# Hybrid decoder step on one core: early weights, conditioning units and idle products put in a new order

## The chip, the cores and the metric

The kernel runs on 1 core of a Trainium2 chip. The metric is the device time of one execution in microseconds (us). Times before: 1947.58 median of 3 runs (1947.49 to 1947.77).

## The reference, cut to what matters

One layer of a decoder trunk on 512 prompt tokens and 8 sample tokens (520 in all), D_MODEL 2048, all in float32. The change touches only the first step: the conditioning of the normalised input, and the first columns of the input projection.

```
def _modulate(x, c, g_norm, w_ada, b_ada):
    mod = c @ w_ada + b_ada
    shift, scale, gate = jnp.split(mod, 3, axis=-1)
    h = _rms(x, g_norm) * (1 + scale[:, None, :]) + shift[:, None, :]
    return h, gate

def _project_in(h, w_in, pos):
    z = h @ w_in
    ...
    q, k, v, qi, ki, wi, ga, u, gb, ma, mb = parts
```

`c` has 9 rows (1 prompt, 8 samples); `w_ada` is 2048 x 6144, `w_in` 2048 x 13456. Behind it come the sparse attention with its indexer, the pooling mixer, the gated merge, the output projection and the final RMS norm.

## The kernel before, in words

**Products in three parts.** A float32 product with a weight tile is done as three products of a faster format: weights high x input high, weights high x input low, weights low x input high. So each 2048 x 128 weight tile (1 MB) passes three steps: a DMA into `raw[p]` (`load`, L344), ACT's cast to `whi[p]` (`hi`, L657), and GpSimd's (POOL's) subtraction into `wlo[p]` (`lo`, L529). There are two such buffers, p = 0 and 1. The input stands in `act_hi` and `act_lo` (16 slices of 128 rows, 520 columns). TensorE's helper `tile` (L1611) runs the products into `acc[p]`.

**The front.** Four token tiles are transposed on TensorE (`token_columns`, L1686) into `H`. Meanwhile `w_ada`'s shift and scale parts (32 units of 1 MB) flow through a ring of SBUF slots. `cond_unit(u)` (L1624) multiplies unit u with the 9 rows of `c`. Four units make a chunk of 512 columns; the order is ADA_CHUNKS: chunks 0 to 3 are scale, 4 to 7 shift. After a chunk ACT copies its sums out of PSUM (`mod_rows`, L695), TensorE turns them into columns (`mod_columns(c)`, L1657), and VectorE and ACT make four slices of the input: VectorE scales `H` (L1047), ACT casts to `act_hi` (L704), VectorE subtracts to `act_lo` (L1032). `scale_rows` (L1694) and `table_columns` (L1645, L1646) prepare the row factors and small tables.

**Early tiles.** While the units stream in, four tiles of the projection (columns of `mb`) are computed from the scaled input without shift, as `early tile` 0 to 3; a later correction adds what the shift makes of them. Tiles 0 and 1 are done in quarters: `early_quarter(e, g)` takes the four slices of group g (24 products), and waits for `act_lo` slice by slice. Tile 0 uses buffers p = 1, tile 1 buffers p = 0. Tiles 2 and 3 follow in one piece each (`tile(*early_at(2), ...)`), with the later units between their parts.

**Slots.** The first units lie in slots that overlay the early tiles' buffers: slot 0 is `raw[0]`, slot 2 `whi[0]`, slot 4 `wlo[0]`. The units from LATE on use five late slots, four of them over the token tiles (`x_tok`), one over `xs`; so SP waits for the transposes (`xT_done`) and ACT's squares (`ss_ready`) ahead of unit LATE, and each later unit waits until the former one of its slot is used (`ring_done`).

**Order.** All queues are written out by hand. SP issues, in one queue: constants, x, units 0 and 1, early tile 0's weights, units 2 and 3 (FIRST_RING has three slots, so unit 3 is the first late one), then it waits for unit 2 to be used and issues early tile 1's weights, then units 4 to 31 with the further early weights between. TensorE's program is one list: units 0 to 2, `scale_rows`, `table_columns`, unit 3, `mod_columns(0)`, then units 4 to 19 with the quarters behind the units that `quarters_after` names; `mod_columns(1)` to `(3)` stand directly behind units 8, 12 and 16. Each engine works through its list in order.

Of the kernel before, what the change touches and what calls it, by code (L numbers as in the profile page):

```python
# [56 lines left out]
ADA_CHUNKS = [4, 5, 6, 7, 0, 1, 2, 3]  # L57
RING = 6
ADA_UNITS = 4 * len(ADA_CHUNKS)
FIRST_RING, LATE_RING = (2, 4, 0), 4  # L60
LATE = len(FIRST_RING)


# [53 lines left out]
def build(nc, t, out):  # L117
# [11 lines left out]
    def at(name, off, shape, dt=F32):  # L129
        size = int(np.prod(shape[1:])) * (2 if dt == BF16 else 4)  # L130
        assert off + size <= 229368 - BASE, (name, off, size)
        return nc.alloc_sbuf_tensor_at(name, shape, dt, offset=BASE + off)
# [9 lines left out]
    ident = at("ident", A0, [P, P])  # L142
# [148 lines left out]
    acc = [ctx.enter_context(nc.psum_tensor(f"acc{p}", [P, 2, 512], F32)) for p in range(2)]  # L291
# [17 lines left out]
    S = sem  # L309
# [5 lines left out]
    def cols(w, c):  # L315

        return w[:, bass.ds(c, P)].rearrange("(k p) n -> p k n", p=P)
# [9 lines left out]
    def early_at(e):  # L327

        return ((e + 1) // 2, 1 - e % 2)
# [8 lines left out]
    def _(sp):  # L338
        def load(q, p, src, first=False):
            if not first:  # L340
                sp.wait_ge(lo_ready[p], q - 1 + p)
            k, n = src.shape[1], src.shape[2]
            dst = raw[p][:, 0:k * n].rearrange("p (k n) -> p k n", n=n)
            sp.dma_start(dst, src).then_inc(raw_landed[p], 16)  # L344

        def load_ada(u):

            former = [v for v in range(u) if RING_AT[v] == RING_AT[u] or RING_SEM[v] == RING_SEM[u]]
            if former:
                sp.wait_ge(S("ring_done"), former[-1] + 1)  # L350
            sp.dma_start(ring[RING_AT[u]][:].rearrange("p (k n) -> p k n", n=512),
                         quarter(w_ada, u % 4, 512 * ADA_CHUNKS[u // 4])).then_inc(stage_landed[RING_SEM[u]], 16)

        def load_early(e, first=False):
            load(*early_at(e), cols(w_in, C_MB + P * e), first=first)
# [9 lines left out]
        sp.dma_start(pgi[:], t["page_table"].rearrange("(o b) n -> o b n", o=1).broadcast_to([P, NB, PAGES])  # L365
                     ).then_inc(S("pages_landed"), 16)
        for u in range(ADA_UNITS):
            if u == 2:
                load_early(0, first=True)
            if u == LATE:  # L370
                sp.wait_ge(S("xT_done"), 8)
                sp.wait_ge(S("ss_ready"), 4)
            if u == LATE + 1:
                sp.wait_ge(S("ring_done"), LATE)
                load_early(1, first=True)
            if u == LATE + LATE_RING:
                sp.wait_ge(S("front_T"), 2)
                sp.wait_ge(S("ss_ready"), 5)
            if u == 17:
                load_early(2)  # L380
            if u == 20:
                load_early(3)
            if u == 27:
                load(Q_A, 1, cols(w_in, C_KI))
            load_ada(u)
# [1187 lines left out]
    def _(pe):  # L1573
        mm = nc.tensor.matmul
# [44 lines left out]
        def cond_unit(u):  # L1619

            c = u // 4
            pe.wait_ge(stage_landed[RING_SEM[u]], 16 * (RING_USE[u] + 1))
            for k in range(4):
                last = mm(ps[32 * k:32 * k + 32, c % 2, :], cWide[:, 4 * (u % 4) + k, :],  # L1624
                          ring[RING_AT[u]][:, k * 512:(k + 1) * 512],
                          start=(u % 4 == 0), stop=(u % 4 == 3))
            last.then_inc(S("ring_done"), 1)

        def early_quarter(e, g):

            tile(*early_at(e), 0, parts=S("act_lo_ready"), free=False, ks=range(4 * g, 4 * g + 4))
# [11 lines left out]
        def table_columns():  # L1643
            pe.wait_ge(S("tables_landed"), 8 * 16)
            tr(ps[:, 3, 16:64], rows_b[:], ident[0:48, 0:48])  # L1645
            tr(ps[:, 3, 64:88], rows_gs[:], ident[0:24, 0:24]).then_inc(S("front_T"), 1)  # L1646

        def mod_columns(c):

            pe.wait_ge(S("mod_rows"), c + 1)  # L1650
            if c == 0:
                pe.wait_ge(S("xs_ready"), 1)
            else:
                pe.wait_ge(S("H_ready"), max(4 * c - 7, 1))
            part, g = divmod(ADA_CHUNKS[c], 4)
            for m in range(4):
                last = mm(modT[g][:, part, m, :], modb[c % 2][:, m * P:(m + 1) * P], sum4, start=True, stop=True)  # L1657
            last.then_inc(S("mod_T"), 1)
# [31 lines left out]
        def scale_rows():  # L1690
            pe.wait_ge(S("xT_act"), 4)
            pe.wait_ge(S("diag_ready"), 5)
            for i in range(4):
                mm(acc[0][:, 0, i * P:(i + 1) * P], ones[:], diag[:, i, :], start=True, stop=True)  # L1694
            mm(acc[0][:, 1, 0:NB], ones[0:NB, :], diagS[:], start=True, stop=True).then_inc(S("front_T"), 1)

        def unit(u):
            if u % 4 == 0 and u >= 8:
                pe.wait_ge(S("mod_rows"), u // 4 - 1)
            cond_unit(u)  # L1700
            if u % 4 == 0 and u > 4:
                mod_columns(u // 4 - 1)

        token_columns(0)
# [1 line left out]
        for i in range(1, 4):  # L1706
            token_columns(i)
        pe.wait_ge(S("front_set"), 2)
        for u in range(3):
            unit(u)  # L1710
        scale_rows()
        table_columns()
        unit(3)
        mod_columns(0)
        pe.wait_ge(S("xT_dve"), 4)
        quarters_after = {4: [(0, 0)], 6: [(1, 0)], 9: [(0, 1)], 12: [(1, 1)], 14: [(0, 2)], 16: [(1, 2)],
                          17: [(0, 3), (1, 3)]}
        for u in range(4, 20):
            unit(u)
            for e, g in quarters_after.get(u, ()):  # L1720
                early_quarter(e, g)
# [458 lines left out]
```

## Time and profile before

| What | Value |
| --- | --- |
| Median of the runs | 1947.58 us |
| Profiled execution: its own time | 1951.26 us |
| Profiled execution: span | 1949.4 us |
| TensorE matmul busy (PE) | 1906.1 us, 98% |
| VectorE (DVE), ScalarE (ACT), GpSimd (POOL) busy | 1009.5, 546.1, 910.4 us |
| Chain that ended last | PE 93%, of it line L1611 70% |
| Mean granted clock of TensorE | 0.991 |

The busy share is a mean over stages with different limits; the stretches of the trace tell them apart. PEclk is the granted TensorE clock as a share of 2.4 GHz: 1.00 or 0.50, which is 1.2 GHz. A value in brackets behind an instruction is the idle time of its engine before it, and what ended it. PE's float32 products stand as two records each.

### The profile page before, as it was taken

To read this page: it belongs to the slowest core of one execution; us is meant where nothing else is said; L and a number is where in the kernel's file an instruction comes from. 1 tells how busy PE (TensorE), PEld (TensorE's weight loads), DVE (VectorE), ACT (ScalarE), POOL (GpSimd) and SP (SyncE) were. 2 spreads that over 40 slices of the span, in tenths; PEclk is the share of its full clock that TensorE was granted. 3 is DMA by queue.
4 is the path that set the end of the run, shared out by engine and by line. 5 is a ranking of instruction groups with operands and counts; after the bars stand their busy time and mean duration, and the time that the engine had idled before them with its cause. 6 is when DMAs were issued, how large, how long until landed. Compare 5 with 4: busy or idle time off the path is not lost.

```text
span 1949.4 us, 34601 instructions
## 1 busy us (share of the span) xinstructions
PE 1906.1 (98%) x14468; PEld 1771.6 (91%) x14468; DVE 1009.5 (52%) x1529; ACT 546.1 (28%) x751; POOL 910.4 (47%) x760
## 2 busy tenths in 40 slices
PE   6999999999999999999999999999999999999997
PEld 4679999988999999999999999999999999887775
DVE  4358886677787778774444675425011411142223
ACT  4332322443333333332222121212222411131223
POOL 1135555555454545453444343444665444334442
PEclk7999999999999999999999999999999999999999
DMA  9994434443333232324233353326475655543333
GB/s 322 342 312 107 108 104 123 139 133 115 88 79 97 75 93 74 97 77 132 72 88 88 98 148 102 97 76 173 133 235 174 186 182 172 180 144 131 98 104 131
DMA packets 328257, 264.44 MB, mean 136 GB/s; under 512 B 8747, under 2 KB 275175, under 8 KB 326839
## 3 DMA queue, kind: packets, MB, share of 16 engines
q1 hardware_dynamic: 314719, 232.42, 40.2%
q10 hardware_dynamic: 8320, 13.80, 2.6%
q0 software_dynamic: 5120, 16.77, 2.5%
q8 instruction: 79, 1.29, 0.3%
q14 instruction: 19, 0.16, 0.0%
HBM read 250.89 MB, written 12.54 MB: 135 GB/s over the span
## 4 chain that ended last, share of the span: by engine, by line
PE 93%; DVE 2%; DMA 2%; SPq 1%; ACT 1%; issue 1%; POOL 0%; DVEq 0%; POOLq 0%; ACTq 0%
PE acc L1611 70%; PE ps L2120 9%; PE ps L1876 1%; DMA ring<-in_w_ada 1%; PE ps L1751 1%; PE ps L1892 1%; PE ps L1624 1%; PE acc L1590 1%; PE ps L1864 1%; PE ps L2049 1%; PE acc L2111 1%; PE ps L1797 1%; PE ps L1939 1%; PE acc L1596 1%; PE ps L1807 0%
## 5 line engine op out<-in xcount | busy, mean ns | idle before, releaser
L529 POOL TENSOR_TENSOR wlo<-raw,whi 128x512 fp32r<-128x512 f32 (+1 forms) x612 | 789.2, 1321 | 818.4 <-ACT whi L657 818.4
L1611 PE MATMUL acc<-act_hi,whi 128*128 128x260 f32 (+1 forms) x3520 | 753.1, 290 | 8.0 <-DVE act_lo L1032 3.0
L1611 PE MATMUL acc<-act_hi,wlo 128*128 128x260 f32 (+1 forms) x3520 | 741.3, 287 | 0.0
L1611 PE MATMUL acc<-act_lo,whi 128*128 128x260 f32 (+1 forms) x3520 | 740.1, 287 | 0.0
L1611 PEld LDWEIGHTS acc<-act_hi,whi 128*128 128x128 f32 x3520 | 552.4, 189 | 34.3 <-issue 23.4
L1611 PEld LDWEIGHTS acc<-act_lo,whi 128*128 128x128 f32 x3520 | 550.9, 189 | 0.7
L1611 PEld LDWEIGHTS acc<-act_hi,wlo 128*128 128x128 f32 x3520 | 551.2, 189 | 0.0
L657 ACT CAST whi<-raw 128x2048 fp32r<-128x2048 f32 (+1 forms) x153 | 279.2, 1825 | 950.9 <-PE acc L1611 749.2
L2120 PE MATMUL ps<-whi,act_hi 128*128 128x512 f32 x256 | 102.1, 399 | 0.0
L2120 PE MATMUL ps<-whi,act_lo 128*128 128x512 f32 x256 | 101.1, 395 | 0.0
L2120 PE MATMUL ps<-wlo,act_hi 128*128 128x512 f32 x256 | 101.0, 394 | 0.0
L1477 DVE SCALAR_TENSOR_TENSOR big<-big,acc 128x520 f32<-128x520 f32 x16 | 11.1, 695 | 155.9 <-PE acc L1611 155.9
L567 POOL CAST k_part<-kT 128x512 fp32r (+1 forms) x16 | 9.8, 612 | 135.8 <-PE ps L1892 124.8
L2120 PEld LDWEIGHTS ps<-whi,act_hi 128*128 128x128 f32 x256 | 48.0, 188 | 21.1 <-issue 10.1
L2120 PEld LDWEIGHTS ps<-whi,act_lo 128*128 128x128 f32 x256 | 48.0, 188 | 11.3
L2120 PEld LDWEIGHTS ps<-wlo,act_hi 128*128 128x128 f32 x256 | 48.1, 188 | 11.0
L814 ACT ACTIVATE accS<-ps,misc 128x128 f32<-128x128 f32 (+1 forms) x64 | 32.9, 527 | 80.8 <-DVE misc L1254 80.8
L767 ACT COPY kiTc<-ps 128x512 f32<-128x512 f32 x32 | 35.0, 1093 | 67.1 <-PE ps L1797 67.1
L1346 DVE SCALAR_TENSOR_TENSOR big<-e_back,acc 128x520 f32<-128x520 f32 (+1 forms) x12 | 8.4, 696 | 84.9 <-PE acc L1611 84.9
L1611 PE MATMUL acc<-pool_hi,whi 128*128 128x260 f32 x256 | 52.0, 284 | 0.0
L1611 PE MATMUL acc<-pool_hi,wlo 128*128 128x260 f32 x256 | 51.4, 282 | 0.0
L1611 PE MATMUL acc<-pool_lo,whi 128*128 128x260 f32 x256 | 51.4, 282 | 0.0
(322 smaller groups left out, 2121.9 us busy)
## 6 DMA issues: line engine op xcount, KB each, us to landing
raw<-in_w_in SPq DMA_DIRECT2D x105, 1024.0 KB, 5.8
ring<-in_w_ada SPq DMA_DIRECT2D x32, 1024.0 KB, 11.4
raw<-in_w_a_proj SPq DMA_DIRECT2D x16, 1024.0 KB, 8.0
gate_unit<-in_w_ada SPq DMA_DIRECT2D x16, 1024.0 KB, 7.1
raw<-in_w_out SPq DMA_DIRECT2D x16, 1024.0 KB, 5.1
raw<-in_w_b_proj SPq DMA_DIRECT2D x16, 512.0 KB, 4.3
x_tok<-in_x_prompt SPq DMA_DIRECT2D x4, 1024.0 KB, 9.1
att_dram<-silu_ga ACTq DMA_DIRECT2D x16, 256.0 KB, 2.6
```

The source lines that it names most:

```text
L529: return nc.gpsimd.tensor_tensor(wlo[p][:, a:b], raw[p][:, a:b], whi[p][:, a:b].bitcast(F32), ALU.subtract)
L657: nc.scalar.copy(whi[p][:, 0:n], raw[p][:, 0:n]).then_inc(hi_ready[p], 1)
L767: nc.scalar.copy(kiTc[u % 4][:].rearrange("p (c r) -> p r c", r=4), ps[:, 2 if u else 3, :].rearrange("p (r c) -> p r c", r=4)).then_inc(S ...
L814: last = nc.scalar.activation(prob[:, OFF[b]:OFF[b] + w], ps[:, bank, c:c + w], ACT.Exp, bias=nmq[:, b:b + 1], scale=ATT_SCALE, accum_out= ...
L1590: mm(o, whi[p][:, k * P:(k + 1) * P], x[:, k, s], start=(k == 0 and x is hi_), stop=False)
L1596: last = mm(o, wlo[p][:, k * P:(k + 1) * P], hi_[:, k, s], start=False, stop=(k == KT - 1))
L1611: last = mm(o, w, x[:, k, s], start=(k == 0 and n == 0), stop=(k == kt - 1 and n == 2))
L1624: last = mm(ps[32 * k:32 * k + 32, c % 2, :], cWide[:, 4 * (u % 4) + k, :], ring[RING_AT[u]][:, k * 512:(k + 1) * 512], start=(u % 4 == 0) ...
L1751: last = mm(ps[:, b - 1, 0:(b + 1) * P], qis[p][:, x, (b - 1) * P:b * P], kis[:, y, 0:(b + 1) * P], start=(n == 0), stop=(n == 2))
L1797: last = tr(ps[:, 2 if u else 3, r * P:(r + 1) * P], kib[u % 3][:, r * P:(r + 1) * P], ident[:])
L1864: last = tr(ps[:, n // 4, (n % 4) * P:(n % 4 + 1) * P], prob[:, OFF[qb] + kb * P:OFF[qb] + (kb + 1) * P], ident[:])
L2120: last = mm(ps[:, i, :], x, w, start=(k == 0 and n == 0), stop=(k == KT - 1 and n == 2))
```

## The change

Slot 0 goes from the first units' list, so that units 0 and 1 lie in slots 2 and 4 and unit 2 is the first late one. SP issues early tile 0's weights ahead of unit 0 and early tile 1's weights behind unit 3; its wait for unit 2 goes, since `raw[0]` no longer holds a unit. POOL's wait (`ring_done`, LATE) ahead of tile 1's low part is now for two units. TensorE's list is rewritten up to unit 8. `keep_running(n)` does n products of the identity with itself into columns of a PSUM bank that nothing reads: 33 in all. TensorE's wait for VectorE's last token copy (`xT_dve`) moves ahead of the first of them. `scale_rows` and `table_columns` stand behind unit 1, `mod_columns(1)` behind unit 7 and twelve idle products, and the quarters behind other units.

```diff
@@ -57,7 +57,7 @@
 ADA_CHUNKS = [4, 5, 6, 7, 0, 1, 2, 3]
 RING = 6
 ADA_UNITS = 4 * len(ADA_CHUNKS)
-FIRST_RING, LATE_RING = (2, 4, 0), 4
+FIRST_RING, LATE_RING = (2, 4), 4
 LATE = len(FIRST_RING)
 
 
@@ -365,13 +365,12 @@
         sp.dma_start(pgi[:], t["page_table"].rearrange("(o b) n -> o b n", o=1).broadcast_to([P, NB, PAGES])
                      ).then_inc(S("pages_landed"), 16)
         for u in range(ADA_UNITS):
-            if u == 2:
+            if u == 0:
                 load_early(0, first=True)
             if u == LATE:
                 sp.wait_ge(S("xT_done"), 8)
                 sp.wait_ge(S("ss_ready"), 4)
-            if u == LATE + 1:
-                sp.wait_ge(S("ring_done"), LATE)
+            if u == 4:
                 load_early(1, first=True)
             if u == LATE + LATE_RING:
                 sp.wait_ge(S("front_T"), 2)
@@ -1694,11 +1693,15 @@
                 mm(acc[0][:, 0, i * P:(i + 1) * P], ones[:], diag[:, i, :], start=True, stop=True)
             mm(acc[0][:, 1, 0:NB], ones[0:NB, :], diagS[:], start=True, stop=True).then_inc(S("front_T"), 1)
 
+        def keep_running(n, spare=acc[1]):
+            for _ in range(n):
+                mm(spare[:, 1, 384:512], ident[:], ident[:], start=True, stop=True)
+
         def unit(u):
             if u % 4 == 0 and u >= 8:
                 pe.wait_ge(S("mod_rows"), u // 4 - 1)
             cond_unit(u)
-            if u % 4 == 0 and u > 4:
+            if u % 4 == 0 and u > 8:
                 mod_columns(u // 4 - 1)
 
         token_columns(0)
@@ -1706,16 +1709,29 @@
         for i in range(1, 4):
             token_columns(i)
         pe.wait_ge(S("front_set"), 2)
-        for u in range(3):
-            unit(u)
+        unit(0)
+        pe.wait_ge(S("xT_dve"), 4)
+        keep_running(4)
+        unit(1)
         scale_rows()
         table_columns()
+        unit(2)
+        keep_running(4)
         unit(3)
+        keep_running(5)
         mod_columns(0)
-        pe.wait_ge(S("xT_dve"), 4)
-        quarters_after = {4: [(0, 0)], 6: [(1, 0)], 9: [(0, 1)], 12: [(1, 1)], 14: [(0, 2)], 16: [(1, 2)],
-                          17: [(0, 3), (1, 3)]}
-        for u in range(4, 20):
+        unit(4)
+        keep_running(8)
+        early_quarter(0, 0)
+        unit(5)
+        unit(6)
+        keep_running(6, acc[0])
+        unit(7)
+        keep_running(6, acc[0])
+        mod_columns(1)
+        early_quarter(1, 0)
+        quarters_after = {9: [(0, 1)], 11: [(1, 1)], 13: [(0, 2)], 15: [(1, 2)], 17: [(0, 3), (1, 3)]}
+        for u in range(8, 20):
             unit(u)
             for e, g in quarters_after.get(u, ()):
                 early_quarter(e, g)
```

## Rows read from the trace of the kernel before

**Rows 1.** Page, part 1: busy us, share of the span, instructions.

```profile
PE 1906.1 (98%) x14468; PEld 1771.6 (91%) x14468; DVE 1009.5 (52%) x1529; ACT 546.1 (28%) x751; POOL 910.4 (47%) x760
```

**Rows 2.** Stretches: length, PE, PEld, DVE, ACT, POOL busy, clock, DMA share, GB/s.

```profile
25.40:45.70 20.30, 13.46 (x57) 7.95 (x58) 8.28 (x22) 6.08 (x7) 4.94 (x4) 0.50 0.96 329
...
52.70:56.00 3.30, 3.30 (x17) 3.28 (x16) 0.00 (x0) 0.00 (x0) 0.00 (x0) 0.50 1.05 387
...
62.90:66.20 3.30, 3.30 (x16) 3.00 (x15) 2.51 (x4) 1.22 (x2) 0.00 (x0) 0.50 1.05 388
66.30:93.80 27.50, 27.39 (x224) 19.30 (x223) 12.27 (x24) 9.19 (x13) 1.68 (x2) 1.00 0.98 316
93.80:144.20 50.40, 50.11 (x404) 39.38 (x404) 26.57 (x39) 17.57 (x25) 20.82 (x15) 1.00 0.98 330
```

**Rows 3.** Timeline, 0 to 60 us: start, length, instruction, [idle before <- releaser].

```profile
18.04 1.94 PE L1686 MATMUL acc<-ident,x_tok 128*128 128x128 f32 x16 [1.10 <-ACT H L687]
...
20.77 1.06 PE L1624 MATMUL ps<-ring,cWide 128*32 128x512 f32 x8 [0.79 <-DMA ring<-in_w_ada]
...
23.43 1.07 PE L1624 MATMUL ps<-ring,cWide 128*32 128x512 f32 x8 [1.59 <-DMA ring<-in_w_ada]
...
26.77 1.90 ACT L657 CAST whi<-raw 128x2048 fp32r<-128x2048 f32 x1 [3.47 <-DMA raw<-in_w_in]
...
29.51 1.94 PE L1624 MATMUL ps<-ring,cWide 128*32 128x512 f32 x8 [5.02 <-DMA ring<-in_w_ada]
...
31.51 0.37 SPq L344 DMA_DIRECT2D raw<-in_w_in  x1
...
40.94 1.94 PE L1624 MATMUL ps<-ring,cWide 128*32 128x512 f32 x8 [2.03 <-DMA ring<-in_w_ada]
```

**Rows 4.** Chain that ended last, 18 to 57 us: start, length, what.

```profile
31.45 2.01 PE acc L1694 x8
...
34.47 1.91 PE ps L1624 x8
...
36.40 0.59 ACT modb L695
...
37.04 1.89 PE ps L1657 x8
...
51.57 4.67 PE acc L1611 x24
```

**Rows 5.** Timeline of PE at two waits (49 to 52, 60 to 63 us).

```profile
51.57 0.51 PE L1611 MATMUL acc<-act_hi,whi 128*128 128x260 f32 x2 [2.44 <-POOL wlo L529]
...
62.31 0.48 PE L1611 MATMUL acc<-act_hi,whi 128*128 128x260 f32 x2 [2.24 <-DVE act_lo L1032]
```

**Rows 6.** Chain that ended last, 56 to 95 us.

```profile
58.09 1.00 PE ps L1657 x8
...
61.47 0.71 DVE act_lo L1032
...
62.31 4.84 PE acc L1611 x24
...
73.83 1.85 PE ps L1624 x16
75.68 3.06 PE acc L1611 x24
```

**Rows 7.** Timeline of DVE: third and fourth low slice of group 1.

```profile
64.02 1.47 DVE L1032 TENSOR_TENSOR act_lo<-H,act_hi 128x520 fp32r<-128x520 f32 x2
```

**Rows 8.** Timeline of PE in the attention: one f32 product, then the next.

```profile
715.27 0.38 PE L1877 MATMUL ps<-reluP,vcur 128*128 128x128 f32 x2
715.49 0.39 PE L1888 MATMUL ps<-kT,qiT 128*128 x2
```

**Rows 9.** Timeline of PE: first product of early tile 2.

```profile
93.70 0.50 PE L1590 MATMUL acc<-act_hi,whi 128*128 128x260 f32 x2
```

**Rows 10.** Tile ring, the transfer that SP issued at 76.9: issue to landing.

```profile
DMA to landing us min/median/max: 12.5/12.5/12.5
```

## The prediction, made before the changed kernel ran

> **What bounds the kernel now.** I read part 1 of the page first: TensorE (PE) is busy 98% of the span [rows 1], so a change counts only where it moves PE's own sequence. The change lies in the first 94 us, so next came the table of stretches [rows 2]. The reader is to see two things there. From 25.4 to 45.7 PE ran at a granted clock of 0.50, the lower level of 1.2 GHz, and again in two short stretches up to 66.2. From 66.3 on it runs at 2.4 GHz and is busy 27.39 of 27.50 us, then 50.11 of 50.40. So after 66.3 PE neither waits nor is slowed, though the DMA share there is 0.98: transfers and PE run nearly level, and PE is the one that sets the end. All that can be won lies between 20.0 us, where the last token transposes end, and 66.3, plus what the new order does up to 93.70, the first product of the third early tile [rows 9], which I take as the finish line: what follows it is the same program, with PE full, and I carry a shift there through to the end one for one.
>
> The timeline then shows the losses. PE waits for units 0, 1, 2 and 4 (0.79, 1.59, 5.02 and 2.03 us) [rows 3], for the low part of the second early tile (2.44) and for the first low activation slice of group 1 (2.24) [rows 5]. The 5.02 us stand because the first early tile's weights lie between units 1 and 2: the units start at 20.77 and 23.43, the cast of those weights at 26.77, unit 2 at 29.51. The 2.03 us stand because SP issues the second early tile's weights at 31.51 only, when unit 2 is done [rows 3].
>
> **Prices.** From the rows at 2.4 GHz: two units 1.85, so 0.93 each; mod_columns 0.99; a quarter 3.06 [rows 6]. At 1.2 GHz: unit 1.94 [rows 3], scale_rows with table_columns 3.02 (31.45 to 34.47), mod_columns 1.89 [rows 4]. An idle product is a 128x128 f32 product: at 2.4 GHz such a product in the attention takes 0.22 from its start to the next [rows 8]; at 1.2 GHz four in scale_rows take 2.01, 0.50 each [rows 4]. There are 33 of them, 7.3 or 16.5 us of PE work that was not there. The chain through VectorE: call T0 to T3 the ends of mod_columns 0 to 3. Before, T1 is 59.09 and the first low slice ends at 61.47 + 0.71, T1 + 3.1 [rows 6]; the fourth at 64.02 + 1.47, T1 + 6.4 [rows 7]. A quarter of that group can't start before T + 3.1 nor end before T + 6.4 + 0.8 (its last fourth) = T + 7.2. The second early tile's low part is ready at 51.57 with T0 = 38.93, T0 + 12.6 [rows 4, 5].
>
> **The change part by part, in order of time.**
>
> *First early weights ahead of unit 0.* They take 3.3 us of the stream (23.43 to 26.77) and a unit 2.7. Moved to the front, they put unit 0 at 24.1 and unit 1 at 26.8; unit 2 stays at 29.5, unit 3 lands near 32.2 as before. PE now idles 4.1 us before unit 0, and no more between units.
>
> *Units 0 to 3 with idle products.* At 1.2 GHz: unit 0 to 26.0, 4 idle products 28.0, unit 1 29.9, scale_rows and table_columns 33.0. Where the clock rises no row of before can say, since idle products are not in it. Bounds: at 2.4 GHz throughout, unit 3 is done 33.1, its copy (0.59 and some 0.1 of signals) 33.8, 5 idle products 34.2, T0 = 35.2. At 1.2 throughout, unit 2 34.9, 4 idle 36.9, unit 3 38.8, 5 idle 41.3, T0 = 43.2. I take a rise at 33.0, after 9 us without a gap: unit 2 33.9, idle 34.8, unit 3 35.7, idle 36.8, T0 = 37.8, that is 1.1 earlier than before. The copy is hidden behind the 5 idle products.
>
> *Second early weights behind unit 3, no wait for unit 2.* SP's wait goes. In the stream these weights then follow unit 3 at once: unit 4 at 32.2 + 3.3 + 2.7 = 38.2 or, if they take 1 us more, 39.2; I take 38.7 in place of 40.94. Queued behind on SP are units 4 to 31, which move forward by the same 2.2 us. That they need their ring slots freed by PE is no limit: five slots are ahead.
>
> *Unit 4, 8 idle products, quarter (0,0).* Unit 4 and the idle products take 2.7 us at 2.4 GHz, 5.9 at 1.2; PE has just done mod_columns and waited about 1 us for unit 4, so I can't tell and take the middle, 4.3: 43.0. All low slices of group 0 are there by T0 + 6.4 = 44.2, so the quarter runs through, to 46.1.
>
> *Units 5 to 7, two times 6 idle products, mod_columns(1).* All landed. 2.8 of units, 2.6 of idle products on the path, 1.0: T1 = 52.5. Of each six idle products only the second's hides anything, the copy before mod_columns (0.7). Before, T1 was 59.09, but with quarter (1,0) and unit 8 done; with these (3.06 + 0.93) the new order stands at 56.5, so 2.6 ahead for equal work.
>
> *Quarter (1,0) behind T1.* Its low part is ready at T0 + 12.6 = 50.4: the wait of 2.44 is gone. With units 8 and 9 it also fills the time up to T1 + 3.1, so quarter (0,1) no longer waits 2.24. It ends at 60.5; units 10, 11, quarter (1,1), unit 12, mod_columns(2): T2 = 67.3.
>
> *Quarters after 11, 13, 15 in place of 12, 14, 16.* Here the order takes something back. Before, quarter (1,1) and units 13, 14 stood between mod_columns(2) and quarter (0,2), 4.8 us of work over a chain of 3.1. Now only unit 13 does (0.9): PE waits 2.2 us for the first low slice, then goes at VectorE's pace. The same between mod_columns(3) and quarter (0,3), which has only unit 17 before it. Before, quarter (0,1) stood just so, behind unit 9: it ended at 67.15, T1 + 8.06 [rows 6], more than 7.2 because the clock fell to 0.50 in it [rows 2]. I take 8.06 twice: quarter (0,2) to 75.4, units 14, 15 and quarter (1,2) 80.3, unit 16 and mod_columns(3) T3 = 82.2, quarter (0,3) 90.3, (1,3) 93.3, units 18 and 19 95.2. Without the stall these two quarters would end at T + 4.0, so the new order costs 4.1 each.
>
> A rule speaks against this price. In both waits of before (2.44 and 2.24 us) the granted clock was 0.50 in the stretch after them [rows 2, 5]. The Trainium skill (TensorE: Matmul & The Clock Gate, section "Why this matters for your kernels") warns of longer gaps between bursts than these. By that rule the waits of 2.2 us would leave the clock up, and the quarters end at T + 7.2: 93.5 in place of 95.2. The rows disagree with it here, and I go by the rows.
>
> **The sum.** 95.2 - 93.70 = +1.5 us. Won: 2.6 up to T1. Lost: two stalls, less the one stall of before. On the profiled execution (span 1949.4, its own time 1951.26) that gives 1952.8. The median of the runs shown, 1947.58, lies 3.7 below the profiled one; the same shift gives 1949.1.
>
> **The rivals.**
>
> *The clock stays down until quarter (0,0) (slower).* T0 = 43.2, unit 4 45.1, 8 idle products 49.1, the quarter as long as the one before (4.67 [rows 4]) 53.8, then 6.4 to T1 at 60.2, 7.7 later than in the sum: +9.2, 1956.8. For it: before, PE worked from 29.51 to 36.38 without a gap and the clock stayed at 0.50 [rows 2 to 4]; nearly the same instructions now follow in another order. Against it: the idle products are denser than table_columns or mod_columns, and dense quarters brought the clock back each time. It decides from T1 = 54.9 on, where the shift passes 3.9 us. Half of it (only unit 4 and its idle products at 1.2, 1.6 more) gives 1950.7, still no change.
>
> *The clock holds everywhere.* T0 = 35.2, unit 4 and idle products to 41.4, quarter (0,0) 41.4 to 44.6, T1 = 51.0, and both stalls end at T + 7.2: 1.5 + 1.7 less than the sum, 92.0, -1.7: 1945.9.
>
> *The stream sets the end (faster).* If PE only followed its transfers, closing the hole would count in full. Unit 19 was issued at 76.9 and landed 12.5 later [rows 10], at 89.4. Without holes, 16 units of 2.7 and two early loads of 3.3 behind unit 3 put it at 32.2 + 43.2 + 6.6 = 82.0, 7.4 earlier. That would be 1940.2. For it: DMA share 0.98 [rows 2]. Against: unit 19 was used one unit ahead of 93.70, at 92.8, 3.4 after it landed, and PE's work up to there doesn't shrink.
>
> *The moved load does nothing.* If SP, held by a full queue, still gets unit 4 in at 40.9, that is 2.2 later in the sum: T1 = 54.7, 1951.3.
>
> **How the numbers follow.** Two thousandths of the time, 3.9 us, is about what a measurement can tell from no change: 1943.7 to 1951.5. The sum and its milder clock variants, 1947 to 1951.3, hold 0.62; the clock that holds 0.12; the load without effect 0.03; the clock down until the quarter or most of the way 0.16; the stream 0.07. So faster 0.07, same 0.75, slower 0.18 (the slow clock, and a little of the upper end of the sum). The range reaches from 1945.6, just below the case with the clock up, to 1952.8, about halfway to the slow-clock case.
>
> **What would show it.** Unit 0 starting near 24 and unit 4 near 38.7, SP's load of the second early tile issued before 31.5. T0 near 38 and T1 near 52.5. Waits of about 2.2 us on act_lo ahead of the quarters behind units 13 and 17, with a granted clock of 0.50 behind them, and none ahead of the quarter behind unit 9. The third early tile starting near 95.2. It is wrong if the clock up to 43 is other than said, if those two waits are missing, or if something after the finish line gives a shift back.

## The result and the profile after

Measured side by side, 14 runs each: 1953.35 us median (1951.63 to 1955.55) for the changed kernel, 1948.49 (1946.66 to 1950.85) for the kernel before; ratio 1.0021 with a 95% interval of 1.0014 to 1.0029, so 2.7 to 5.7 us slower. Applied to the 1947.58 of the prediction, the ratio gives 1951.7, inside its range of 1945.6 to 1952.8. The forecast was +1.5, in the class of no change (two thousandths); the measurement lies at the border of that class, on the slow side. The profiled execution took 1952.72 with a span of 1950.9, both 1.5 above the profiled execution before; its third early tile starts at 96.52 in place of 93.70 [rows 9], 2.8 later.

The stretches of the changed kernel (length, busy time of the engines, granted clock, DMA share, GB/s), to be read beside [rows 2]:

```profile
26.30:36.20 9.90, 7.96 (x62) 4.93 (x59) 4.47 (x15) 0.67 (x2) 4.95 (x4) 1.00 1.10 353
36.40:43.00 6.60, 4.96 (x22) 3.30 (x23) 4.88 (x8) 4.30 (x5) 0.39 (x1) 0.50 1.05 387
43.20:70.30 27.10, 25.64 (x211) 18.06 (x209) 8.38 (x19) 4.36 (x8) 4.42 (x4) 1.00 1.03 374
70.50:77.10 6.60, 6.01 (x28) 5.47 (x32) 3.69 (x6) 1.63 (x3) 0.00 (x0) 0.50 1.11 343
77.40:87.40 10.00, 7.76 (x66) 4.72 (x59) 3.33 (x8) 1.83 (x3) 0.00 (x0) 1.00 1.03 320
87.60:90.80 3.20, 3.20 (x15) 3.06 (x15) 2.60 (x5) 1.25 (x2) 0.00 (x0) 0.50 1.05 387
91.00:144.00 53.00, 53.00 (x434) 41.19 (x433) 22.11 (x35) 19.71 (x26) 20.04 (x16) 1.00 0.92 296
```

The clock is up through the first units, which it was not before. Three stretches stand at 1.2 GHz: one over unit 4 and its eight idle products (unit 4 ran at 1.2 GHz before too), and one around each of two waits at quarters (0,2) and (0,3), which is new. From 91 on PE is full without a gap. What PE waited for in the first 200 us (total, times, longest):

```profile
PE ps L1623 <- DMA ring<-in_w_ada: 6.5, 4, 3.1
PE acc L1610 <- DVE act_lo L1031: 5.5, 3, 2.2
```

The wait of 2.4 us for the low part of the second early tile is gone [rows 5]; the waits for act_lo have grown from one long one to two. PE's and SP's timeline of the changed kernel shows where they stand (the view of unit 0 ends at 24 us and so counts five of its eight records):

```profile
22.29 0.51 SPq L344 DMA_DIRECT2D raw<-in_w_in  x1
...
23.56 1.02 PE L1623 MATMUL ps<-ring,cWide 128*32 128x512 f32 x5 [2.27 <-DMA ring<-in_w_ada]
...
34.02 0.96 PE L1656 MATMUL ps<-misc,modb 128*128 128x9 f32 x8
...
38.04 1.94 PE L1623 MATMUL ps<-ring,cWide 128*32 128x512 f32 x8 [3.06 <-DMA ring<-in_w_ada]
...
71.08 0.77 PE L1610 MATMUL acc<-act_hi,whi 128*128 128x260 f32 x2 [2.24 <-DVE act_lo L1031]
...
87.10 0.48 PE L1610 MATMUL acc<-act_hi,whi 128*128 128x260 f32 x2 [2.24 <-DVE act_lo L1031]
...
96.52 0.50 PE L1589 MATMUL acc<-act_hi,whi 128*128 128x260 f32 x2
```

SP now issues the second early tile's weights at 22.29 (before: 31.51), mod_columns(0) ends at 34.98, and unit 4 starts at 38.04 (40.94 in [rows 3]). The chain of the changed kernel from 40 to 97 us gives the lengths (start, length, what); L1698 is the idle products:

```profile
39.98 3.50 PE acc L1698 x16
43.47 2.88 PE acc L1610 x24
46.34 1.85 PE ps L1623 x16
48.20 1.54 PE acc L1698 x12
49.73 0.99 PE ps L1623 x8
50.73 1.54 PE acc L1698 x12
52.27 0.79 PE ps L1656 x8
53.06 2.95 PE acc L1610 x24
...
62.79 3.07 PE acc L1610 x24
...
66.86 1.00 PE ps L1656 x8
...
71.08 5.54 PE acc L1610 x24
76.62 2.17 PE ps L1623 x16
...
82.88 1.00 PE ps L1656 x8
...
87.10 7.63 PE acc L1610 x48
```

mod_columns 1, 2 and 3 end at 53.06, 67.86 and 83.88. Quarter (0,2) takes 5.54 behind its wait, where a free one takes 3.07; quarters (0,3) and (1,3) take 7.63 for two. Eight idle products at 1.2 GHz take 3.50, six at 2.4 GHz 1.54.

### The profile page after: what moved, and what is told of

It is laid out like the page before. It is cut to its first block, busy times and chain, and to the rows that moved or that the text cites. A ratio compares the mean times of both kernels' runs of the same rounds, so it can differ in the third digit from the quotient of the medians.

```text
span 1950.9 us, 34732 instructions
## 1 busy us (share of the span) xinstructions
PE 1911.8 (98%) x14534; PEld 1778.7 (91%) x14534; DVE 1009.9 (52%) x1529; ACT 545.9 (28%) x751; POOL 907.8 (47%) x760
## 3 DMA queue, kind: packets, MB, share of 16 engines
q1 hardware_dynamic: 314719, 232.42, 40.3%
## 4 chain that ended last, share of the span: by engine, by line
PE 94%; DMA 2%; DVE 2%; ACT 1%; issue 1%; POOL 0%; SPq 0%; DVEq 0%; ACTq 0%
PE acc L1610 70%; PE ps L2136 9%; PE acc L1589 1%; PE ps L1623 1%; PE ps L1892 1%; PE ps L1767 1%; PE ps L1908 1%; PE ps L1880 1%; DMA ring<-in_w_ada 1%; PE acc L2127 1%; PE ps L2065 1%; PE ps L1813 1%; PE ps L1955 1%; PE acc L1595 1%; PE ps L1823 0%
```

## The experiments

All times are set against runs of the kernel before on the same chip in the same comparison.

**The quarters put back behind units 12, 14, 16.**

```diff
-        quarters_after = {9: [(0, 1)], 11: [(1, 1)], 13: [(0, 2)], 15: [(1, 2)], 17: [(0, 3), (1, 3)]}
+        quarters_after = {9: [(0, 1)], 12: [(1, 1)], 14: [(0, 2)], 16: [(1, 2)], 17: [(0, 3), (1, 3)]}
```

> The changed kernel with the quarters of before behind units 12, 14 and 16 in place of 11, 13 and 15; all else as changed. Theory 1 (the two stalls behind mod_columns 2 and 3 are the main loss): quarter (0,2) and (0,3) no longer wait and run in 3.1 us each, the changed kernel took 7.8 and 6.8 with their waits; the third early tile starts near 88.1 in place of 96.5, and the time is 4 to 5.6 us below the kernel before (less than 5.6 only if the stream then sets the pace). Theory 2 (the transfers set the pace, the stalls are time in which units land anyway): the waits move to the units, the third early tile starts at 95 to 97, time 4 us above before.

Ratio to before 0.9982 (0.9973 to 0.9991), median 1946.56. Stretches of this version, then the start of the third early tile and of the indexer's weight product:

```profile
37.00:43.00 6.00, 4.53 (x20) 2.87 (x21) 4.79 (x8) 4.30 (x5) 0.00 (x0) 0.50 1.05 387
43.50:142.00 98.50, 97.44 (x807) 73.90 (x810) 47.11 (x78) 30.97 (x44) 27.38 (x20) 1.00 1.00 338
```

```profile
87.88 0.50 PE L1589 MATMUL acc<-act_hi,whi 128*128 128x260 f32 x2
...
140.63 0.65 PE L1668 MATMUL ps<-H,wiW 128*32 128x260 f32 x8
```

Both waits and both slow stretches behind them are gone, and the tile starts at 87.88 in place of 96.52: the places of these quarters cost 8.6 us there, as theory 1 had it. In time it is 3.5 us below before (1.8 to 5.3), a little less than the 4 to 5.6 expected. Part of that is seen late in its trace: at 910.9 PE waits 2.4 us for the state load of the pooling mixer, which the changed kernel waits 0.8 for (1.7 in its second trace) and the kernel before not at all:

```profile
910.87 0.43 PE L1942 MATMUL ps<-ident,state 120*128 120x120 f32 x2 [2.39 <-DMA state<-in_state_pool]
```

**The two runs of six idle products left out.**

```diff
-        keep_running(6, acc[0])
         unit(7)
-        keep_running(6, acc[0])
```

> The changed kernel without the two runs of six idle products around unit 7. Theory 1 (they lie on TensorE's path and hide nothing but the copy): mod_columns 1 ends 2.3 to 3.0 us earlier than the 53.1 of the changed kernel, the third early tile starts near 94, time 1 us above before, within 1.5. Theory 2 (they hold the clock and so pay for themselves): a stretch at 1.2 GHz appears between 46 and 66 us and eats the 3.0 us; start of the third early tile 96 or later.

Ratio 1.0002 (0.9993 to 1.0011). The third early tile starts at 94.15, 2.4 earlier than in the changed kernel, and mod_columns(1) now waits 0.70 for ACT's copy. It ends at 51.37, 1.7 earlier, for the 2.3 to 3.0 expected, mostly since unit 4 came 0.4 later in this execution. No slow stretch came between 46 and 66 us. So these twelve hold nothing; they only lengthen the path, by 3.1 less the 0.7 that they covered.

**No idle products at all.**

```diff
-            for _ in range(n):
+            for _ in range(0):
```

> The changed kernel without any of its 33 idle products. Theory 1 (those around unit 7 and the eight behind unit 4 only lengthen the path): T1 at 48.8 to 50 in place of 53.1, third early tile at 92 to 93.5, time 0 to -1.5 us against before, even if the clock falls before unit 4. Theory 2 (the idle products of the first units hold the clock): the granted clock is 0.50 from 26 to 43 as in the kernel before, T0 at 38 to 41 in place of 35.0, T1 at 52 to 55, third early tile 95 to 98.

Ratio 0.9994 (0.9984 to 1.0003). Theory 1 came out in all its numbers. Of theory 2 only the clock did, and not its ends of mod_columns 0 and 1. The clock was down in the first units:

```profile
24.80:34.80 10.00, 8.94 (x44) 3.46 (x36) 2.19 (x11) 0.42 (x1) 4.94 (x4) 0.50 1.09 350
38.50:41.60 3.10, 3.08 (x13) 1.43 (x14) 3.07 (x6) 1.88 (x3) 0.00 (x0) 0.50 1.05 387
```

```profile
36.03 1.06 PE L1656 MATMUL ps<-misc,modb 128*128 128x9 f32 x8 [0.71 <-ACT modb L694]
```

T0 comes at 37.09 in place of 34.98, so the first 13 idle products do win 2.1 us there (T0 is 36.23 in the other version without any, further down). But unit 4 starts at 38.0 to 38.5 in either version, as it lands, and that hides them. T1 is 49.47 in place of 53.06, the third early tile 92.27 in place of 96.52. Together the 33 idle products cost more than they earn.

**The load order alone, on TensorE's old list.**

```diff
-FIRST_RING, LATE_RING = (2, 4, 0), 4
+FIRST_RING, LATE_RING = (2, 4), 4
...
-            if u == 2:
+            if u == 0:
                 load_early(0, first=True)
...
-            if u == LATE + 1:
-                sp.wait_ge(S("ring_done"), LATE)
+            if u == 4:
                 load_early(1, first=True)
```

> The kernel before with only the load order of the change (first early weights ahead of unit 0, second behind unit 3, slots 2 and 4 for the first units); TensorE's list as before. Theory 1 (the stream is not what sets the end): unit 4 starts near 39 in place of 40.94, but quarter (1,0) still waits for its low part until T0 + 12.6, near 51.5, so T1 stays at 58.5 to 59.1 and the time is within 1 us of before. Theory 2 (closing the hole in the stream counts in full): third early tile 2 to 7 us earlier than 93.7, time the same amount below before.

Ratio 0.9994 (0.9985 to 1.0003): no change in time. In the trace unit 4 starts at 38.82, T0 is 36.81 and the third early tile starts at 91.63, 2.1 earlier, against the 0 that I expected; T1 is 56.9, not 58.5 to 59.1. Quarter (1,0) waited for its low part just as theory 1 said, T0 + 12.65:

```profile
49.46 0.51 PE L1610 MATMUL acc<-act_hi,whi 128*128 128x260 f32 x2 [2.39 <-POOL wlo L528]
```

So the whole shift came from T0, and that came from the clock, which in this execution stayed up until 30 and was up again for unit 3 and mod_columns(0). Whether that belongs to the load order is taken up by the last experiment.

**Old quarters without idle products, without the sixes, and with the first 13 only.** All three have the quarters as in the first experiment; the first two also have the edit of the second or third. The last one leaves out the eight idle products behind unit 4 as well as the sixes:

```diff
         unit(4)
-        keep_running(8)
         early_quarter(0, 0)
```

> The changed kernel with the quarters of before behind units 12, 14 and 16, and without any idle product. Theory 1 (stalls and idle products are separate terms on TensorE's path and add up): the third early tile starts at 87.9 - 4.25 = 83.6, and that carries through: the weight product of the indexer (wi) starts near 136.4 and the time is 10 us below before. Theory 2 (with the stalls gone the stream takes over as the bound, since units 21 and 31 already lay only 0.3 us ahead of their use): the tile starts at 83.6 to 85, but TensorE then waits for units 20 to 31 in w_ada's ring, 3 us or more in all; unit 31 can't land before 124, so wi starts at 139 to 140.6 and the time is within 1 us of that of the version with the old quarters alone.

> The changed kernel with the quarters of before and without the two runs of six idle products. Theory 1 (terms add up): third early tile at 87.9 - 2.4 = 85.5, wi near 138.3, time 2.4 us below the version with the old quarters alone. Theory 2 (the stream takes over): third early tile at 85.5, wi at 139 to 140.6, waits for the ring of 1 to 2 us behind unit 20, time within 1 us of that version.

> The changed kernel with the quarters of before, and of the idle products only the 13 among units 0 to 3. Theory 1 for the clock (these hold it at 2.4 GHz up to mod_columns 0, the eight behind unit 4 only run at 1.2 and cost what they last): T0 at 35 to 35.5, quarter (0,0) starts at 40.3 to 40.7 and T1 ends at 48 to 49; third early tile 83 to 84, bounded behind it by the stream as in the version without idle products. Theory 2 (the eight bring the clock back for the quarter and pay for themselves): quarter (0,0) runs at 1.2 GHz for 1 us or more longer, T1 at 50 or later.

| Old quarters and | ratio to before | third early tile | wi product |
| --- | --- | --- | --- |
| all 33 idle products | 0.9982 (0.9973 to 0.9991) | 87.88 | 140.63 |
| 21 (no sixes) | 0.9978 (0.9969 to 0.9988) | 86.39 | 140.70 |
| 13 (first units) | 0.9972 (0.9961 to 0.9982) | 85.80 | 139.13 |
| none | 0.9974 (0.9964 to 0.9984) | 86.31 | 139.53 |

Up to T1 the terms add up (49.26 with 13, 49.85 with none, 53.39 with all). Behind it they don't: the tile starts at 86.31, not at 83.6, and wi moves by 1.1 us of the 4.25. PE's waits from 56 to 142 us in the version without idle products:

```profile
PE ps L1623 <- DMA ring<-in_w_ada: 2.5, 3, 1.0
```

They were 0 in the version with old quarters and all idle products. Theory 2 holds in the main: with the stalls and the idle products both gone the stream takes over, though from unit 12 on already (0.90 there, 0.95 at unit 17, 0.61 at unit 21) and not, as I wrote, only from unit 20. Its third early tile came later than the 83.6 to 85 expected, and by the ratios its time is 1.6 us below the version with all idle products, not within 1 us, though their intervals overlap. In the version without the sixes these waits are 1.2 us, and its tile and wi follow. The four ratios lie within 0.0010 of each other, inside their intervals. The eight idle products behind unit 4 are not seen to buy time either. In the version without them quarter (0,0) took 4.6, mostly at 1.2 GHz, where it takes 2.9 behind them; that much of theory 2 came true. But the eight last 3.5, and T1 is 49.26 without them. Quarter (0,0) started at 39.25, ahead of the 40.3 to 40.7 expected, because in this execution the clock stayed up over unit 4; the third early tile came at 85.80, behind the 83 to 84 expected. The last two have the lowest ratios, some 5 us below the kernel before.

**The new quarters alone, on the old kernel.**

```diff
-        quarters_after = {4: [(0, 0)], 6: [(1, 0)], 9: [(0, 1)], 12: [(1, 1)], 14: [(0, 2)], 16: [(1, 2)],
+        quarters_after = {4: [(0, 0)], 6: [(1, 0)], 9: [(0, 1)], 11: [(1, 1)], 13: [(0, 2)], 15: [(1, 2)],
                           17: [(0, 3), (1, 3)]}
```

> The kernel before with only the new places of the quarters (1,1), (0,2), (1,2): behind units 11, 13, 15 in place of 12, 14, 16. Theory 1 (the stalls come from the places alone): TensorE waits about 2.2 us for act_lo ahead of quarters (0,2) and (0,3), each of which then takes 4.8 us or more; the third early tile starts 7 to 8.6 us later than 93.7, time 7 to 8.6 us above before. Theory 2 (the stalls came of the earlier units and are not there with the old front): the tile starts within 2 us of 93.7.

Ratio 1.0045 (1.0031 to 1.0058), 6 to 11 us slower. The two waits stand in its trace as in the changed kernel's, beside the 2.25 at quarter (0,1) that the kernel before had anyway:

```profile
73.88 0.77 PE L1611 MATMUL acc<-act_hi,whi 128*128 128x260 f32 x2 [2.24 <-DVE act_lo L1032]
88.56 0.48 PE L1611 MATMUL acc<-act_hi,whi 128*128 128x260 f32 x2 [2.25 <-DVE act_lo L1032]
...
97.43 0.50 PE L1590 MATMUL acc<-act_hi,whi 128*128 128x260 f32 x2
```

The tile starts 3.7 later than 93.7, not the 7 to 8.6 expected, because T1 came 3.8 earlier (55.27 for 59.08); from T1 on the list takes 42.2 in place of 34.6, 7.6 more. The time agrees with theory 1, the single trace only if T1 is taken out. Each of the two quarters ran a little faster than the 4.8 expected: behind the wait at 88.56 the clock stayed up.

**Both kernels once more, unchanged.**

> The kernel before, unchanged, profiled once more, to see how far one execution's front differs from another's. Theory 1 (the clock's stretches fall differently in each execution): mod_columns 0 ends between 36.6 and 39 and the third early tile starts between 91.5 and 95; the two versions with the old start of TensorE's list had 36.6 and 36.8 against 38.9. Theory 2 (the front repeats): 38.9 and 93.7 again, within 0.3.

> The changed kernel, unchanged, profiled once more. Theory 1: mod_columns 0 ends at 35 to 35.6, since idle products hold the clock there in every trace so far; the third early tile starts between 95 and 97.5, moved by where the two stalls let the clock fall. Theory 2 (the front repeats): 96.5 again, within 0.3.

The kernel before, a second time: T0 37.32, T1 55.97, third early tile at 89.99, so 3.7 earlier than in the trace that the prediction was read from, and earlier than the 91.5 to 95 of theory 1. Its wait at quarter (0,1), the start of that tile, and its granted clock around both:

```profile
59.21 0.48 PE L1611 MATMUL acc<-act_hi,whi 128*128 128x260 f32 x2 [2.25 <-DVE act_lo L1032]
...
89.99 0.50 PE L1590 MATMUL acc<-act_hi,whi 128*128 128x260 f32 x2
```

```profile
44.40:90.00 45.60, 41.13 (x331) 28.50 (x330) 18.41 (x36) 12.70 (x19) 6.55 (x6) 1.00 1.07 368
```

The same wait of 2.25, and the clock stayed up. Its T0 lies 0.5 from the load-order version's 36.81, so most of that shift needs no help from the load order. From 89.99 the version with only the new quarters is 7.4 later, as its theory 1 had it. The changed kernel, a second time: T0 35.10, the tile at 96.44, within 0.1, with 1.2 GHz around both stalls again:

```profile
70.50:77.00 6.50, 5.90 (x28) 5.47 (x32) 3.70 (x6) 1.64 (x3) 0.00 (x0) 0.50 1.12 344
87.60:90.70 3.10, 3.10 (x15) 2.98 (x15) 2.54 (x4) 1.23 (x2) 0.00 (x0) 0.50 1.05 387
```

So the kernel before has a front that varies with its clock, by at least 3.7 us, and the trace that I worked from showed a late one; the changed kernel repeated itself in its two traces.

## Why the prediction came out as it did

The kind of change was right: won up to T1, lost again at two stalls, a small sum. Its size came out too small: the sum was +1.5, the profiled finish line says +2.8, the runs say +2.7 to +5.7. By its steps:

- **Units 0 to 3.** Unit 0 at 24.1 (23.56) was right. T0 at 37.8 was wrong (34.98): I let the clock be down until 33, and with the idle products it stayed up until 36.2. It made no difference, since unit 4 (38.7; 38.04) covers it.
- **Unit 4 with eight idle products.** 4.3 forecast, the mean of both clocks; 5.2 measured (38.04 to 43.23), nearly all at 1.2 GHz. PE had waited 3.06 for unit 4, not 1.
- **The sixes.** 1.3 forecast each, 1.54 measured: 0.5 us in all. T1 52.5 against 53.06.
- **Quarter (1,0) and (0,1).** Their waits went, as said; T1 to T2 was 14.8 in both.
- **The stalls.** Place, releaser and length (2.2) were right to 0.1. Quarter (0,2) ended at T2 + 8.76, for the 8.06 taken, and the clock fall reached units 14 and 15 (2.17 for 1.85); quarter (0,3) ended near T3 + 7.8. Together 0.8 more than forecast. Moving these quarters back alone gained 8.6 us at the finish line, for the two times 4.1 of the prediction, and moving them forward in the kernel before lost 6 to 11 us in time. So this is the term that decided.
- **The rule on gaps.** I went by two rows against the Trainium skill (TensorE: Matmul & The Clock Gate, section "Why this matters for your kernels"). In the changed kernel the clock fell at both waits again, in two traces; in the second trace of the kernel before it did not, behind the same 2.25. Over all traces PE waited 2.2 to 2.5 us ahead of a quarter 16 times; 14 times the granted clock was 0.50 within 1.7 us of the wait's end, twice it stayed at 1.00. So the rule, read as a promise for shorter gaps, does not hold, and my two rows were no proof of the opposite, though they pointed the right way.
- **Carried through one for one.** This did not hold to the microsecond. In the profiled pair the shift of 2.8 at the finish line is 2.3 at 715 us (the product of [rows 8] starts at 717.54) and 1.5 at the end of the span. Near 900 us it lost 1.4: behind a wait of 3.07 the kernel before ran at 1.2 GHz (899.3 to 902.4), the changed kernel at 2.4 GHz. Its wait of 0.8 for the state load gave part of that back. That the profiled pair differs by just the +1.5 of the sum is therefore luck.
- **The base.** The rest of the gap to the runs is, as far as the traces show, the kernel before. Its second trace reaches the finish line at 89.99; from there the changed kernel is 6.5 later, from the first 2.8, and the runs' 2.7 to 5.7 lies between the two, to 0.1. The own times of these two traces, 1951.26 and 1947.48, differ by about as much as their fronts. The sign was there to be read: the profiled execution lay 3.7 above the median of the runs, and I put the same shift on both. A base from one trace was the mis-sized term that I had not listed. How often each front occurs was not measured.

Of the rivals, the clock that stays down until quarter (0,0) and the load without effect fell at once (clock 1.00 up to 36.2, unit 4 at 38.04). The clock that holds everywhere failed at the stalls. The stream as the bound was false for this change. It stayed false with the stalls alone taken out (no wait for a unit from 56 to 142 us) and came true with idle products gone as well.

## What to carry to other kernels

Where a step starts a chain through other engines (here 3.1 us to the first slice, 6.4 to the last), count the work between it and the first consumer in the engine's list; three quarters moved forward by one unit each cost 8.6 us. Idle products that hold a clock pay only where they fill a wait and the time that they win is not hidden by something else: here a unit's landing hid the 2.1 us that they won. And read a base from two traces before summing single microseconds: the front before differed by 3.7 us between two executions of one program.

## What the runs showed of the hardware

- With 13 idle products among the first units the granted clock was 1.00 from 26.3 to 36.2, in both traces of the changed kernel; without any it was 0.50 from 24.8 to 34.8.
- Eight idle products directly behind unit 4 ran at 1.2 GHz almost to their end, 3.50 us for the eight; the clock rose between 43.0 and 43.2, as the next quarter began (43.23).
- A PE wait of 2.2 us went with 1.2 GHz in the changed kernel both times in both traces, and with 2.4 GHz in the second trace of the kernel before; over all traces 14 of 16 such waits went with 1.2 GHz. A wait of 3.07 near 900 us was followed by 1.2 GHz in the first trace of the kernel before and by 2.4 GHz in the first of the changed kernel.
